# Issuing the cache-to-output copies at the start of the first FFN instead of inside the second input projection

## What is computed

```python
hp = hp + yp
hs = hs + ys
hp = hp + swiglu(rms_norm(hp, norm_g[layer, 1]), w_ffn_gate[layer], w_ffn_up[layer], w_ffn_down[layer])
hs = hs + swiglu(rms_norm(hs, norm_g[layer, 1]), w_ffn_gate[layer], w_ffn_up[layer], w_ffn_down[layer])
```

```python
ext = jnp.concatenate([buf.astype(new.dtype), new], axis=1)
...
bufs.append(ext[:, T:])
```

## Time and profile before

| | us |
|---|---|
| three executions: median (range) | 6021.24 (6009.43 to 6033.26) |
| the profiled execution: span from the first to the last instruction | 6033.6 |
| ffn0: first weight load issued, last tanh of `ffn_hidden` ended | 1888.4, 2425.6 |
| c_in: first matmul, last matmul | 2901.7, 3091.9 |
| rope: first DMA issued | 3119.5 |

### The profile page before, as it was taken

How to read it: one execution, slowest core, us unless ns; L and a number is a source line. 1 busy time by engine, 2 the same in 40 slices (tenths; PEclk the granted TensorE clock), 3 DMA queues, 4 the chain that set the end, 5 groups by cost and what they waited for, 6 DMA issues and landing times. The chain is left out here.

```text
span 6033.6 us, 73045 instructions
## 1 busy us (share of the span) xinstructions
PE 4278.5 (71%) x24716; PEld 3863.5 (64%) x24716; DVE 1626.4 (27%) x3775; ACT 960.7 (16%) x2140; POOL 1118.9 (19%) x684
## 2 busy tenths in 40 slices
PE   2997145456265999996744667888885665999997
PEld 2997134345154999885644656777774364999886
DVE  2002322234433111002032215566563323111001
ACT  1000033201201000001000113344442201000001
POOL 3342200000023333001420002221110022333000
PEclk9999555556577999997875765689997786999998
DMA  3222511511331111121673111110002231111222
GB/s 111 94 82 77 165 55 49 194 46 56 116 122 57 42 45 42 63 66 42 232 260 83 56 50 27 25 25 21 21 19 70 77 112 60 42 44 43 65 66 79
DMA packets 412072, 452.63 MB, mean 75 GB/s; under 512 B 123041, under 2 KB 370434, under 8 KB 408854
## 3 DMA queue, kind: packets, MB, share of 16 engines
q1 hardware_dynamic: 320666, 271.73, 14.7%
q10 hardware_dynamic: 76828, 120.79, 6.3%
q0 software_dynamic: 14448, 58.48, 2.8%
HBM read 370.45 MB, written 153.41 MB: 87 GB/s over the span
## 5 line engine op out<-in xcount | busy, mean ns | idle before, releaser
L383 PE MATMUL ffn_hid_ps<-ffn_x_hi,ffn_hid_w_hi 128*128 128x352 f32 x2112 | 690.9, 327 | 69.9 <-DVEq L415 30.0
L283 PE MATMUL ffn_down_ps<-ffn_down_w,ffn_hT 128*128 128x256 f32 x3168 | 691.1, 381 | 26.4 <-DMA ffn_down_w<-in_w_ffn_down 23.9
L383 PE MATMUL ffn_hid_ps<-ffn_x_lo,ffn_hid_w_hi 128*128 128x352 f32 x2112 | 682.3, 323 | 0.0
L383 PE MATMUL ffn_hid_ps<-ffn_x_hi,ffn_hid_w_lo 128*128 128x352 f32 x2112 | 681.7, 323 | 0.0
L283 PEld LDWEIGHTS ffn_down_ps<-ffn_down_w,ffn_hT 128*128 128x128 f32 x3168 | 605.0, 191 | 112.3 <-issue 27.1
L383 PEld LDWEIGHTS ffn_hid_ps<-ffn_x_hi,ffn_hid_w_hi 128*128 128x128 f32 x2112 | 398.6, 189 | 95.2 <-issue 53.3
L383 PEld LDWEIGHTS ffn_hid_ps<-ffn_x_hi,ffn_hid_w_lo 128*128 128x128 f32 x2112 | 398.7, 189 | 0.0
L383 PEld LDWEIGHTS ffn_hid_ps<-ffn_x_lo,ffn_hid_w_hi 128*128 128x128 f32 x2112 | 398.3, 189 | 0.0
L1831 PE MATMUL nsa_p_psO<-nsa_p_vrow,nsa_p_pT 128*128 128x64 f32 x2112 | 326.7, 301 | 44.5 <-ACTq L1738 36.9
L1831 PEld LDWEIGHTS nsa_p_psO<-nsa_p_vrow,nsa_p_pT 128*128 128x128 f32 x2112 | 293.0, 212 | 95.0 <-ACTq L1738 75.3
L366 POOL TENSOR_TENSOR ffn_hid_w_hi<-ffn_hid_w,ffn_hid_zero 128x1024 fp32r<-128x1024 f32 x88 | 166.8, 1895 | 668.0 <-PEq L386 650.5
(11 more groups left out here) (482 smaller groups left out, 7631.7 us busy)
## 6 DMA issues: line engine op xcount, KB each, us to landing
out<-in_cache_a_kv ACTq DMA_DIRECT2D x8, 4088.0 KB
ffn_hid_w<-in_w_ffn_gate SPq DMA_DIRECT2D x44, 512.0 KB, 3.8
ffn_hid_w<-in_w_ffn_up SPq DMA_DIRECT2D x44, 512.0 KB, 3.9
ffn_down_w<-in_w_ffn_down ACTq DMA_DIRECT2D x8, 2816.0 KB, 10.5
z_ab<-ab_in_o SPq DMA_DIRECT2D x90, 218.0 KB, 2.0
ab_in_w<-in_w_in_ab POOLq DMA_DIRECT2D x10, 1744.0 KB, 8.0
dil_s_kv<-in_cache_a_kv SPq DMA_DIRECT2D x16, 1024.0 KB, 32.6
cmp_pg<-in_cache_c_cmp_kv SPq DMA_DIRECT2D x128, 128.0 KB, 2.1
```

What stands on the lines that cost most here:

```text
L283: last = nc.tensor.matmul(ps[:, q % BANKS, 0:n], x[:, k, t * P:(t + 1) * P], y[:, s, k, :], start=(k == 0 and m == 0), stop=(k == kc - 1 a ...
L383: last = nc.tensor.matmul(ps[:, g, m, 0:N], w[:, m, k, :], x[:, k, cols], start=(k == 0 and n == 0), stop=(k == KD - 1 and n == 2))
```

## The change

`keep_rows` becomes one unrolled list of all 32 copies, without a loop register. It is given to the first FFN's `ffn_hidden` as `meanwhile`, which ACT runs ahead of its loop, and no longer to c_in's `project`.

```diff
-def ffn_hidden(nc, tag, xT, lo, wg, wu, hT):
+def ffn_hidden(nc, tag, xT, lo, wg, wu, hT, meanwhile=None):
...
             @block.scalar
             def _(act):
+                if meanwhile is not None:
+                    meanwhile(act)
                 with act.Fori(0, KF // WS) as i:
...
-        N_C, TURN = 460, 2
-        SEQS = DEC_B * N_C * TURN // IN_C
-        assert SEQS * IN_C == DEC_B * N_C * TURN
-
-        def keep_rows(eng, i):
-            for n in range(SEQS):
-                b = bass.ds(i * SEQS + n, 1)
+        N_C = 460
+
+        def keep_rows(eng):
+            for b in range(DEC_B):
                 for to, of, w in keep:
                     eng.dma_start(to[b, 0:w - DEC_T], of[b, DEC_T:w]).then_inc(kept, 16)
...
-        ffn("ffn0", 0, hid[1], hid[2])
+        ffn("ffn0", 0, hid[1], hid[2], keep_rows)
...
-        mixer_in("c", hid[2], k["gain10"], i["w_in_c"][0], z_c, N_C, keep_rows)
+        mixer_in("c", hid[2], k["gain10"], i["w_in_c"][0], z_c, N_C)
```

More of the change, by code:

```diff
@@ L2406, in mixer_out, with ffn @@
                 project(nc, f"{tag}_out", hi[:], kc, w, out, 256, resid=h, lo=lo[:])
-        def ffn(tag, layer, h, out):
+        def ffn(tag, layer, h, out, meanwhile=None):
             with nc.sbuf_tensor(f"{tag}_hT", [P, KF, ROWS], F32) as hT:
@@ L2411, in ffn @@
                     norm_transpose(nc, f"{tag}_norm", h, k[f"gain{layer}1"], k["ident"], hi[:], lo[:], spare=hT[:])
-                    ffn_hidden(nc, f"{tag}_hid", hi[:], lo[:], i["w_ffn_gate"][layer], i["w_ffn_up"][layer], hT[:])
+                    ffn_hidden(nc, f"{tag}_hid", hi[:], lo[:], i["w_ffn_gate"][layer], i["w_ffn_up"][layer], hT[:], meanwhile)
                 project(nc, f"{tag}_down", hT[:], KF, i["w_ffn_down"][layer], out, 256, resid=h)
```

## The result

| | before | after |
|---|---|---|
| median of runs, us | 6025.62 (6009.43 to 6033.26, 4 runs) | 6123.44 (6117.24 to 6130.42, 4 runs) |
| span of the profiled execution, us | 6033.6 | 6125.2 |
| ffn0: first weight load issued to last tanh of `ffn_hidden` starting | 1888.45 to 2425.13 = 536.7 | 1888.04 to 2549.19 = 661.2 |
| c_in: first eviction by ACT to rope's first DMA | 2908.38 to 3119.47 = 211.1 | 3033.03 to 3214.43 = 181.4 |

The changed kernel is slower: 1.0164 times the time before, 95% interval 1.0147 to 1.0181. The forecast was 6122 us and +101. The two medians differ by 97.8, the two spans by 91.6. Of the spans' difference ffn0 makes 124.5 more; c_in takes 28.5 less from its first matmul to rope's first DMA (29.7 less from its first eviction on); the other stages together are 4.4 us shorter, 3.4 of it behind rope's first DMA, which no run here explains.

The account below looks back on a forecast made before the run. The prediction took PE to bound ffn0, its weight loads hidden by about 3 us, and copy-delayed stores to hold c_in's end. +132 in ffn0 and -31 in c_in gave +101: 6021.24 + 101 = 6122 us, 8-in-10 range 6075 to 6155.

Parts of the forecast that it names:

- The loss in ffn0: In ffn0, weight loads caught beside the copies make PE wait: +132 us with the cold start, ends 122 and 140.
- One packet per queue and turn: DMA engines take one packet of each queue in turn, whatever its size: 1.75 us per turn, 114 us per weight load.
- a sign: While the copies run in ffn0, about 1890 to 2040 us, q1's packet count equals q10's.
- several packets per turn: Rival, chance 0.12: in ffn0 an engine takes about 9 small load packets per turn; about 6040 us.
- hidden loads: Rival, chance 0.05: no weight load in ffn0 is late, so only c_in's gain counts; 5990 us.
- How long the copies last: All 32 copies, 48.0 MB beside ffn0, take 150 us, so their queue is empty at about 2039.
- the two ways: In ffn0 either the first weight load slips through, PE 123 us late, or it is caught too, 135 us late.
- the second way: In ffn0 the first weight load is caught too, and PE begins its second half-block 135 us late.
- The cold start: PE grows cold while waiting in ffn0 and restarts at a lower clock: some 2 us.
- Issuing on ACT: ACT spends 25 us issuing 32 copies before ffn0's first tanh; costs nothing, up to 10 us if loads were not late.
- What c_in gives back: Without copies c_in's stores land sooner and rope begins earlier: -31 us, ends -24 and -32.
- gives nothing back: Rival, chance 0.08: something other than the stores holds rope's start, so c_in's -31 is lost; 6153 us.

Follow-up runs that it names:

- The kernels with one and two sequences at a time: Changed kernel with its 32 copies issued behind ACT's tanh in ffn0's early passes: one sequence per pass, 6016.24 us; two sequences every second pass, 6077.21 us.
- the short copies: Changed kernel with each of its 32 copies cut to 16 rows, moving 0.9 MB instead of 48: 5996.86 us, 0.9958 of the time before.

## Why the prediction was right

The forecast was +101 and 6122 us; the median is 6123.44. That it lies only 1.4 us off is luck. The loss in ffn0 was put 7.5 us too high and the gain in c_in 2.5 too high, which partly cancel; the difference is 97.8 us by the medians and 91.6 by the spans; and the four runs of the changed kernel spread over 13 us. The mechanism is what was right.

- **One packet per queue and turn.** Right: 1058 against 1040 packets where the earlier trace rows had 548 each, now with packets of 512 bytes, the case that the prediction said the trace of before did not show for long. It held while both queues had work, from the second load to the end of the copies; over the whole stretch the counts are not equal, unlike what the prediction named as a sign, because the first load slipped through and the third ended behind the copies. A load took 113.2 us, predicted 114. The rivals with several packets per turn and with hidden loads are out. The Trainium skill (DMA: Bandwidth & Descriptors, Queues, rings and completion order) would have had an engine drain 9 to 17 descriptors before it switches; the counts here, 1058 against 1040, show one profiled packet.
- **How long the copies last.** Predicted to about 2039; q10's 1408 packets lie between 1889 and 2042, and the third split, whose load ended behind the copies, starts at 2040.32.
- **The loss in ffn0.** Predicted +132, measured +124.5. Of the two ways that the prediction left open it was the first: the first load slipped through (split at 1892.84), the second and third were caught. That way had been worked out at 123 late, with the cold start 125, and the third split's products were ready for PE at 2040.32 + 4.4 = 2044.7, 122 behind the 1922.82 of the earlier trace rows. Of the 1 us between, 0.7 is the step from landing to split, which the prediction put at 0.8 us: it is 0.1, before (the load issued at 1896.98 took 4.7 us, its split started at 1901.80) as after (2015.22, 25.0 and 2040.32). The mis-sized step is the choice of 130, a value nearer the second way, on the ground that both issues fall within a microsecond. The kernels with one and two sequences at a time show the same again: each load issued within 0.1 us of a burst's first copy went through, seven of seven and three of three (such as 1961.64 against 1961.68, and 2021.73 against 2021.69); the two issued 3.6 and 3.3 us behind it were caught. In each of these bursts the smallest copy goes first; whether a large first copy would let a load through was not tried.
- **The cold start.** Predicted 2 us; the third half-block met a granted clock of 0.80 and the next had 1.00. 124.5 less 122 leaves 2.5 us for this and the rest.
- **Issuing on ACT.** Predicted 25 us and hidden; it took 33.7 (1887.71 to 1921.43) and was hidden: PE waits 14.2 us for DVE's products in the whole stage, 15.0 before. The prediction added that up to 10 us would show if the loads were not late; with the short copies they were not, ACT issued for 21.4 us, and ffn0 took 0.5 us more than before. The difference to 25 is in the last issue, which alone took 11.46 us (the 59.57 us of idle time again begin in the stage ahead):

```profile
1907.12 2.83 ACTq L2391 DMA_DIRECT2D out<-in_cache_a_kv  x3
1909.97 11.46 ACTq L2391 DMA_DIRECT2D out<-in_cache_c_win_kv  x1
1921.68 1.28 ACT L398 ACT_TABLE_LOAD   x1 [59.57 <-issue]
```

- **What c_in gives back.** Predicted -31 (ends -24 and -32), measured -28.5. The prediction's pace of 5.01 us per tile was 5.08: 34 tiles from 3033.03 to 3205.76. From the last tile to rope's first DMA it is 3214.43 - 3210.78 = 3.65, predicted 3.6. The rival "gives nothing back" is out.

## What to carry to other kernels

Before a large DRAM-to-DRAM copy is put beside a stage because that stage asks for few bytes, count packets, not bytes: here a load that was issued behind the copies waited one packet of theirs for each small one of its own, as long as the copies' queue was not empty. What such a burst costs is its length less the time for which PE still has weights (14 to 26 us here, some 10 to 12 where a load was issued a few us behind the burst's start). So cut the copy into pieces shorter than that and spread them over the stage; 56 pieces of at most 1 MB cost ffn0 nothing here where 32 copies in one go cost 124.5 us. Small packets issued in one go move the cost to the engine that issues them; spread over eight passes they cost ffn0 1.0 us.

## What was not expected of the hardware

An issue took much longer when much was already waiting in the queue: the 32nd copy held ACT for 11.46 us, while three issues just before it took 2.83, and when it was through, 1117 of q10's 1408 packets were still to start. With the short copies the 32nd issue took 0.61 us. With packets of about 1 KB, 32 issues of half as many bytes held ACT from the start of the stage until 1959.45, and in the kernel with 1 KB packets and one sequence per pass ACT is held in eight places, 134.6 us in all:

```profile
ACT ffn_hid_e L394 <- issue: 134.6, 8, 17.5
```

That cost next to nothing, as ffn0's 537.7 us show: the longest of these waits, 17.5 us, is far from the 76.9 us of the kernel that issued all in one go. How many packets a queue takes before it holds its engine was not measured.
